# A compression network turned round: its inputs held by TensorE, its weights streamed, and its units put between the key and value tiles

## What is computed

```python
q, kc, vc, ks, vs, kw, vw, gates = _split(h @ w_in, [NSA_N_HEADS * DH] + [NSA_KV_DIM] * 6 + [3 * NSA_N_HEADS])
...
def nsa_compress(t, pos, w1, w2):      # t: (1, 256, 4 groups, 128)
    sub = t.reshape(bsz, seq // NSA_CMP_STRIDE, NSA_CMP_STRIDE, g, d)
    blocks = jnp.concatenate([sub[:, :-1], sub[:, 1:]], axis=2) + pos[None, None, :, None, :].astype(t.dtype)
    flat = jnp.moveaxis(blocks, 3, 2).reshape(bsz, blocks.shape[1], g, NSA_CMP_BLOCK * d)
    return jax.nn.silu(flat @ w1) @ w2
```

## Time and profile before

| | us |
|---|---|
| median of 3 runs | 2659.84 (2658.85 to 2662.68) |
| the profiled execution, its own time | 2655.95 |
| its span, first to last instruction | 2654.3 |
| PE busy in the span | 2620.2 (99%) |
| DVE, ACT, POOL busy | 1799.1, 1426.6, 220.8 |

### The profile page before, as it was taken

How to read it: one execution, slowest core, us unless ns; L and a number is a source line. 1 busy time by engine, 2 the same in 40 slices (tenths; PEclk the granted TensorE clock), 3 DMA queues, 4 the chain that set the end, 5 groups by cost and what they waited for, 6 DMA issues and landing times. The chain is left out here.

```text
span 2654.3 us, 46566 instructions
## 1 busy us (share of the span) xinstructions
PE 2620.2 (99%) x15363; PEld 2288.2 (86%) x15363; DVE 1799.1 (68%) x2612; ACT 1426.6 (54%) x2210; POOL 220.8 (8%) x195
## 2 busy tenths in 40 slices
PE   7999999999999999999999999999999999999999
PEld 6888888888888888888888888888888888888888
DVE  7677777765677777775555765665777777775444
ACT  5676767654455555554444445655555555554443
POOL 0122112222100000000111001001300000000000
PEclk9999999999999999999999999998999999999999
DMA  5655555656555555556666555222555555556665
GB/s 186 211 203 193 197 189 198 197 173 187 180 192 188 189 190 190 190 186 184 189 188 197 184 182 195 94 93 88 190 183 188 186 188 189 190 190 185 188 188 168
DMA packets 135255, 481.96 MB, mean 182 GB/s; under 512 B 15104, under 2 KB 17152, under 8 KB 134160
## 3 DMA queue, kind: packets, MB, share of 16 engines
q1 hardware_dynamic: 132480, 467.72, 54.9%
q0 software_dynamic: 2336, 12.65, 1.4%
q10 hardware_dynamic: 368, 0.65, 0.1%
HBM read 478.80 MB, written 2.16 MB: 181 GB/s over the span
## 5 line engine op out<-in xcount | busy, mean ns | idle before, releaser
L980 DVE TENSOR_TENSOR w_lo<-raw,w_hi 128x1024 fp32r<-128x1024 f32 x900 | 1099.8, 1224 | 695.8 <-ACT w_hi L359 694.8
L692 PE MATMUL ps<-xn,w_hi 128*128 128x512 f32 x4768 | 1509.4, 398 | 11.0 <-DVE xn L1006 9.6
L359 ACT ACTIVATE w_hi<-raw 128x1024 fp32r<-128x1024 f32 x900 | 938.1, 1044 | 867.8 <-PE ps L694 848.1
L694 PEld LDWEIGHTS ps<-xn,w_lo 128*128 128x128 f32 x4768 | 897.3, 188 | 212.3
L694 PE MATMUL ps<-xn,w_lo 128*128 128x256 f32 x4768 | 938.4, 278 | 0.0
L692 PEld LDWEIGHTS ps<-xn,w_hi 128*128 128x128 f32 x4768 | 728.4, 189 | 19.5 <-DVE xn L1006 10.3
L692 PE MATMUL ps<-hid,w_hi 128*128 128x512 f32 x1408 | 446.9, 395 | 0.0
L694 PEld LDWEIGHTS ps<-hid,w_lo 128*128 128x128 f32 x1408 | 264.7, 188 | 57.1
L694 PE MATMUL ps<-hid,w_lo 128*128 128x256 f32 x1408 | 288.0, 279 | 0.0
L692 PEld LDWEIGHTS ps<-hid,w_hi 128*128 128x128 f32 x1408 | 219.6, 189 | 5.4
L692 PE MATMUL ps<-y_ssm,w_hi 128*128 128x512 f32 x512 | 161.6, 397 | 0.0
(11 more groups left out here) (240 smaller groups left out, 1783.2 us busy)
## 6 DMA issues: line engine op xcount, KB each, us to landing
raw<-w_gu SPq DMA_DIRECT2D x352, 512.0 KB, 3.6
raw<-w_ssm_in SPq DMA_DIRECT2D x162, 512.0 KB, 3.6
raw<-w_down SPq DMA_DIRECT2D x128, 448.0 KB, 3.4
raw<-w_nsa_in SPq DMA_DIRECT2D x82, 512.0 KB, 3.6
raw<-w_ssm_out SPq DMA_DIRECT2D x64, 512.0 KB, 4.4
raw<-w_down SPq DMA_DIRECT2D x64, 512.0 KB, 3.6
raw<-w_nsa_out SPq DMA_DIRECT2D x32, 512.0 KB, 3.5
wcum<-cum_scratch POOLq DMA_DIRECT2D x8, 1024.0 KB, 8.0
```

The source lines that it names most:

```text
L359: act.activation(w_hi[:, slot, 0:n * P], raw[:, slot, 0:n * P], ACT.Copy).then_inc(unit_rounded, 1)
L692: pe.matmul(acc[:, 0:2 * n], w_hi[:, slot, cols], x[:, kb, 0:2 * n], start=(kb == 0), stop=False)
L694: mm = pe.matmul(acc[:, n:2 * n], w_lo[:, slot, cols], x[:, kb, 0:n], start=False, stop=(kb == p.blocks - 1))
L980: TT(w_lo[:, slot, 0:n * P], raw[:, slot, 0:n * P], w_hi[:, slot, 0:n * P].bitcast(F32), ALU.subtract).then_inc(unit_split, 1)
```

## The change

`kvs` and `cmp` become one phase of 48 units (`Woven`), the same list on each engine, without loops. From tile 3 on, one or two compression units stand behind most tiles. Key tiles come first (`KVS_ORDER`).

```diff
+KVS_ORDER = [0, 1, 2, 3, 8, 9, 10, 11, 4, 5, 6, 7, 12, 13, 14, 15]
+CMP_GAPS = [3, 4, 5, 5, 6, 7, 8, 8, 9, 10, 11, 11, 12, 13, 14, 14]
+FOLD_BANK = [2, 6]
...
+        for k in range(tiles):
+            self.order += [(k, 0), (k, 1)]
+            for _ in range(gaps.count(k)):
+                self.order.append((None, at))
```

```diff
-                for b in range(UNIT):
-                    kb = (v % 4) * UNIT + b
...
+                acc = ps[7][0:CMP_N, 0:T].rearrange("p (m n) -> p m n", m=2)
+                for b in range(4):
+                    l = u % 8 * 4 + b
+                    rows = cin[i][:, l * CMP_N:(l + 1) * CMP_N]
+                    hi, lo = (w[:, slot].rearrange("p (m n) -> p m n", m=2)[:, :, b * P:(b + 1) * P] for w in (w_hi, w_lo))
+                    pe.matmul(acc, rows, hi, start=(l == 0), stop=False)
+                    mm = pe.matmul(acc, rows, lo, start=False, stop=(l == CMP_L - 1))
                 mm.then_inc(unit_used, 1)
+
+            def cmp_fold(i):
+
+                pe.wait_ge(fold_set, 1)
+                pe.wait_ge(cmp_copied, i + 1)
+                if i:
+                    pe.wait_ge(kstd_ready, 1)
+                for f in range(2):
+                    mm = pe.matmul(ps[FOLD_BANK[i]][:, f * KVG * NCMP:(f + 1) * KVG * NCMP], halves[i][:, f * P:(f + 1) * P],
+                                   fold[0:CMP_N], start=True, stop=True)
+                mm.then_inc(cmp_folded, 1)
```

```diff
+            steps = {9: lambda: cmp_fold(0), 10: key_sums, 13: key_scales}
...
+            cmp_fold(1)
+            turn_values(0)
...
                     elif v == 0:
+                        turn_values(1)
+                        turn_values(2)
+                    elif v == 1:
+                        turn_values(3)
                         compressed()
-                    elif v == 2:
+                    elif v == 3:
                         pe.wait_ge(ksq_ready, 5)
                         pe.matmul(ps[6][:, P:P + KVG * NCMP], ones[:], kcsq, start=True, stop=True).then_inc(kss_done, 1)
-                    elif v == 3:
+                    elif v == 4:
                         turn_gates()
```

```diff
+            steps = {4: lambda: key_square(0), 5: lambda: key_square(1), 8: lambda: key_square(2), 9: lambda: key_square(3),
+                     10: lambda: cmp_silu(0), 11: key_std}
             for v in range(p.body):
...
+                if v == 3:
+                    cin_round(0)
+                if v == 5:
+                    cin_round(1)
```

```diff
-            for i in range(2):
-                dve.memset(cin[i][:, CMP_L * CMP_N:].bitcast(F32), 0.0)
...
+                split_unit(p.unit0 + RING + v, UNIT)
+                if v in p.ends(0):
+                    k = p.ends(0)[v]
+                    tile_sum(p, 0, k, kv[:, 8 + KVS_ORDER[k]])
+                    if k == 11:
+                        key_roots()
+                    if k in (13, 14):
+                        norm_keys(2 * k - 26)
+                        norm_keys(2 * k - 25)
+                if v < 4:
+                    cin_form(v // 2, 2 * (v % 2))
+                    cin_form(v // 2, 2 * (v % 2) + 1)
+                if v in (4, 6):
+                    cin_rest(v // 2 - 2)
...
-                    elif v == 0:
-                        norm_keys(3)
-                    elif v == 2:
+                    elif v == 3:
                         dve.wait_ge(vcmp_done, 1)
```

More of the change, by code:

```diff
@@ L108, in trunk @@
     last = None
-    for name, blocks, tiles, dram, first, per, *more in (
+    for name, blocks, tiles, dram, *more in (
             ("dt", 16, 1, w_ssm_in, 0, 1), ("ssm", 16, 80, w_ssm_in, 1, 10, [1, 5, 6, 7, 0]),
@@ L203, in trunk @@
             kcsq = q[:, 8, 0:KVG * NCMP]
+            halves = [q[0:CMP_N, 9 + i] for i in range(2)]
+            fold = sb("fold", [P, KVG * NCMP], F32, st)
             krs = sb("krs", [P, 4 * KVG], F32, st)
@@ L592, in _, with key_square @@
[L592 to L614 removed]
+            def key_square(n):
+                act.wait_ge(cin_ready, 2)
+                act.wait_ge(tile_out, ph["kvs"].tile0 + 2 * n + 2)
+                act.activation(ksq[n], keys[n], ACT.Square).then_inc(ksq_ready, 1)
@@ new lines, in key_sums, with key_scales @@
+            def key_sums():
+                pe.wait_ge(ksq_ready, 4)
+                for a in range(4 * KVG):
+                    mm = pe.matmul(ps[6][:, a:a + 1], ksq[a // 4][:, (a % 4) * L:(a % 4 + 1) * L], ones[:, 0:1], start=True, stop=True)
+                mm.then_inc(kss_done, 1)
+            def key_scales():
+                pe.wait_ge(kdiag_ready, 1)
+                pe.wait_ge(chid_ready, 1)
+                for n in range(4):
+                    pe.matmul(ps[2 + n][:], ones[:], kdiag[:, 4 * n:4 * n + 4], start=True, stop=True).then_inc(kbc_done, 1)
@@ new lines, in turn_values @@
+            def turn_values(g):
+                pe.wait_ge(tile_out, ph["kvs"].tile0 + 12 + g + 1)
+                pe.wait_ge(k_ready, g + 1)
+                for a in range(4):
+                    tile = (12, 20)[a // 2] + g
+                    mm = pe.transpose(ps[2 + g][:, a * P:(a + 1) * P], kv[:, tile, (a % 2) * L:(a % 2 + 1) * L], ident[:])
+                mm.then_inc(vt_done, 1)
+            p = ph["kvs"]
+            steps = {9: lambda: cmp_fold(0), 10: key_sums, 13: key_scales}
+            for v in range(p.body):
+                if p.order[v][0] is None:
+                    cmp_unit(p, v, p.order[v][1])
+                else:
+                    gemm_unit(p, 0, v, xn)
+                if v in p.ends(0) and p.ends(0)[v] in steps:
+                    steps[p.ends(0)[v]]()
```

156 lines of the change are left out of this document (81 added, 75 removed).

## The result

| | before | after |
|---|---|---|
| median of 5 runs each, us | 2658.85 (2651.44 to 2662.68) | 2638.31 (2635.77 to 2640.38) |
| ratio, 95% interval | | 0.9929 (0.9912 to 0.9946) |
| span of the profiled execution, us | 2654.3 | 2634.1 |
| mean granted clock in that span | 0.994 | 0.997 |

As a gain, 13.8 us were forecast, from the 2659.84 of three runs, and 20.5 were measured, from the 2658.85 of five.

The account below looks back on a forecast made before the run. PE, busy 99% of the span, bounds the kernel; -15.05 - 0.1 - 0.45 + 1.0 + 0.2 + 0.8 = -13.6 us, from the median 2659.84 to 2646 us. Range 2639 to 2653.

Parts of the forecast that it names:

- The matmuls, -15.05: Compression on PE: inputs held, weights streamed, 128 fewer matmuls at an unchanged spacing of 0.1176 us, -15.05 us.
- rival 2: Compression matmuls: the 120-column load is not overlapped, spacing 0.224 us or more, 2670 us, slower; chance 0.04.
- The folds, +1.0: Two folds on PE, each 2 f32 matmuls of 60 columns in two passes, 0.48 us each: +1.0 us.
- DVE at the start, +0.2: Start of the tiles: two memsets gone, -0.3, input differences moved up, PE waits at tile 4, +0.5; net +0.2 us.
- Query body 0, +0.8: Compressed values' copy stands behind a DVE tile sum; PE waits 1.1 to 1.2 us at the gates' transpose, before 0.3.
- The wait at 1617, -0.45: PE's wait before 1617.43, ascribed to ACT being late with side work, goes away: -0.45 us.
- POOL: hidden: POOL's diagonal of the key scales, 3.6 us, follows tile 11, due after tile 13, 13.9 us later: hidden.
- The clock, 0 with bounds of 1.7: After the one-column key sums, the same 3.4 us half-clock stretch, costing 1.7, is expected again: 0; bounds -1.7 and +1.7.
- The loads, 0: Compression loads in 2 KB runs among tiles: 263 GB/s over 41.8 us, landing 3.9, over 5 us spare: 0.
- rival 1: Dense stretch: loads set the pace; at 240 GB/s +4.1, 2650 us; chance 0.10 with part gain left, 0.03 with none.
- ACT's waits as a sign of trouble: Sign of a wrong forecast: ACT waiting for loads repeatedly between tiles 3 and 14, with PE waiting for splits.
- 117 us from the first key tile to the first query unit: Sign of a right forecast: this stretch takes 117 us in place of 131.6.

Follow-up runs that it names:

- b1: Changed kernel with each compression matmul issued twice, 256 as before the change: 2656.36 us, 1.0006 of the kernel before.
- b2: Changed kernel with DVE's input forming spread singly over eight units and the compressed-values copy one step earlier: 2643.73 us, 0.9951 of the kernel before.
- a1: Changed kernel run again without any edit: 2641.59 us, 0.9953 of the kernel before.
- b4: Changed kernel with the edits of b2 and b3 together: 2639.32 us, 0.9940 of the kernel before.
- a2: Kernel before with key sums 32 and query sums 64 columns wide in place of one: 2649.19 us, 0.9981 of the kernel before.
- a3: Changed kernel with key sums 32 and query sums 64 columns wide in place of one: 2641.22 us, 0.9949 of the kernel before.
- b3: Changed kernel with the key scales' diagonal made by ACT in four pieces after units 34 to 37, not POOL: 2643.09 us, 0.9951 of the kernel before.
- c1: Kernel before with the key scales' diagonal made by ACT behind compression units 9 and 10, not POOL: 2659.26 us, 1.0004 of the kernel before.
- a4: Changed kernel with all 16 compression units behind the last tile, not woven: 2659.48 us, 1.0023 of the kernel before.

## Why the prediction was right, and where not

- **The matmuls, -15.05.** Right. The spacing is 0.118, and b1 puts them back for +13.0, with another 1.5 that went into waits. Loads of 120 columns are as well hidden as those of 128, so rival 2 falls: it wanted over 0.224. The Trainium skill ("TensorE: Matmul & The Clock Gate", Weight-path perf modes) allows the fast weight load only for 128 weights; here the load of 120 lasted 182 ns and that of 128 197 ns, and no run shows a price.
- **The folds, +1.0.** One measured 0.38, so +0.8.
- **DVE at the start, +0.2.** 1.2 at tile 3 and 0.4 at tile 4 as against 1.3 before: +0.3, in the places named, and b2 shows that it is the forming.
- **Query body 0, +0.8.** The wait is 1.1, as worked out.
- **The wait at 1617, -0.45.** Wrong. I put it down to ACT's side work, which set when the split began, but would not have made PE wait. It was a DVE split that stood still under POOL's diagonal (3.18 us in place of 1.21), and the same lock went along: 1.1 us of waits at 1587 and 1588. "POOL: hidden" was the failed step: the diagonal's own 3.6 us are hidden, what it does to DVE is not. The term is +0.65 in place of -0.45.
- **The clock, 0 with bounds of 1.7.** This is the step that made the number miss. The mechanism was right (half clock costs half), but I looked only at the changed stage. There the profiled execution had none, -1.7; and in the attention, which the sum left out, it had 3.6 us at half clock in place of 17.4, -6.0 more. Neither is a gain of the change: that the profiled execution had none was luck. In a1 the stage had two stretches, and the gain was 11 us. The clock's share of this kernel's time moves by 5 us either way from run to run, whatever the change, and the runs that I started from, by their times against later ones of the same kernel (2658.85 to 2662.68 against medians of 2652.65 to 2656.17), had been granted little of it. That these came from another chip is a rival that the record can't rule out; between the chips of the three calls the full-clock time of before differs by 0.9 us at most.
- **The loads, 0.** 248 GB/s over the dense 42 us, 303 over 8; ACT waited for them often between 1495 and 1615, as its waits show, PE not once, so rival 1 falls. I had named ACT's waits as a sign of trouble; alone they were none. But the margin was smaller than the 5 us that I gave it: I took 3.9 us for a landing, and between 1520 and 1562 it was 5.2 and 4.8, and in b4 PE did wait 0.5 us behind a late load. First ACT's waits from 1495 to 1615, then the loads issued between 1520 and 1562 with their medians to landing:

```profile
ACT w_hi L402 <- DMA raw<-w_nsa_in: 12.8, 9, 2.9
ACT w_hi L402 <- DMA raw<-w_cmp: 2.4, 4, 1.4
```

```profile
raw<-w_nsa_in SPq DMA_DIRECT2D x13, 512.0 KB, 5.2
raw<-w_cmp SPq DMA_DIRECT2D x9, 512.0 KB, 4.8
```

- **117 us from the first key tile to the first query unit.** It was 115.7, and the agreement hides an omission: twelve of the sixteen value transposes moved behind the mark, into query body 0, where they take 1.2 us. With them the measured terms give -15.05 - 0.1 + 0.65 - 1.7 + 0.8 + 0.3 - 1.2 = -16.3, and the trace has 115.7 - 131.6 = -15.9. It changes nothing in the forecast time.

Summed with what was measured, from the reciprocal to the first scores: -15.05 - 0.1 + 0.65 - 1.7 + 0.8 + 0.3 + 0.8 = -14.3; the trace has -14.1. Without the clock's -1.7 the same terms give -12.6, and -12.6 is what the change is worth over the whole kernel at full clock, where the sum said -13.6. Between a2 and a3, where the wait at 1617 is not shortened by the clock and is 1617.43 - 1615.95 - 0.12 = 1.4 us, the term for the lock is 1.1 - 1.4 = -0.3 and they give -13.5 (measured: -13.3).

**What stays open.** Why a stretch comes in one execution and not in the next was not found. Where they come can be told: in the thirteen profiles every fall of the clock between 1500 us and the end of the attention starts during, or at most 1.5 us after, a run of narrow sums or a wait of PE (1.3 to 2.9 us). With one-column sums 11 of them stand behind the query sums, in nine profiles; with 64 columns none, in four, and there the four falls in the attention all stand behind waits. That is a pattern and no proof of a cause, since most such places pass without a fall. In the kernel before, wide sums took nearly all of the scatter away; in the changed kernel they did not, and I have no run that tells why. Whether the change itself alters the clock's share is open too: 0.9966 and 0.9952 for it, 0.9945 to 0.9955 for the kernel before.

## What to carry to other kernels

When a product has few inputs and many weights, count the weight loads: holding the narrow side halves the instructions at an unchanged 0.118 us each, but the units become so short that loading, rounding and splitting can't follow, and only putting them between longer units brings the gain home. Before a few us are ascribed to a change, multiply each run's span by its granted clock: here that took a scatter of 14 us down to about 1 and differences of 11 and 20 us to 13.0 and 12.1. A "hidden" POOL instruction with operands in SBUF is not free if DVE has a deadline for a two-operand instruction during it.

## What the runs showed of the hardware that I had not expected

- A DVE instruction with two tensors in SBUF that started 0.55 us after a POOL one took 4.15 us in place of 1.21 and ended 1.08 us after POOL's end; with the diagonal on ACT no split took over 1.23 (b3, c1).
- Stretches of about 3.4 us at half clock, up to three in a row, with PE busy all through them (0.51 at 1707.6, after one-column sums; 0.50 at 1793.0, after a wait of 1.34 us), at some of the same places in one execution and at others of them in the next. The kernel whose PE waited most had most of them in its stage: 20.8 us in a4.
- Key sums of 32 columns cost what those of one column cost: 3.66 and 3.63 us for 32 of them.
- Loads of 512 KB, part of them in runs of 2 KB, held 303 GB/s over 8 us. Over the dense 42 us they landed in 5.2 and 4.8 us (medians), where at 185 GB/s before it had been 3.5.
